# Tokens in step order, and the norm's factor multiplied at the projection's eviction

## The chip, the cores and the metric

The kernel runs on one core of one Trainium2 chip. The metric is the device time of one execution in microseconds (us). TensorE multiplies, VectorE and ScalarE work elementwise, GpSimd (POOL) and SyncE mostly move data here.

## The reference

One inference step of a two-layer hybrid decoder, for a prompt of 256 tokens and eight samples of four tokens, 288 token columns in all, model width 1024, fp32 throughout.

```python
def rmsnorm(x, g):
    y = xf * lax.rsqrt(jnp.mean(xf * xf, axis=-1, keepdims=True) + EPS)
    return (y * g).astype(x.dtype)
# layer 0: h += ab_mixer(rmsnorm(h))   latent attention + gated linear attention, w_out
# layer 1: h += s5_mixer(rmsnorm(h))   diagonal state space over positions, GELU, GLU
def channel_mixer(h, g, w_up, w_down):           # every layer
    a = jax.nn.relu(rmsnorm(h, g) @ w_up)
    return (a * a) @ w_down
def per_layer_embedding(h, p, g, w_gate, w_proj): # every layer
    gate = jax.nn.sigmoid(rmsnorm(h, g) @ w_gate)
    return gate * (p @ w_proj)
```

## The kernel before

The residual h lies in `hT` as eight tiles of 128 features by 288 tokens. A projection sums, for each block of 128 outputs, over the eight tiles in one PSUM bank. The stream of weights comes in units of 1 MB (128 x 2048) through a ring of five buffers; an up unit holds two output blocks, a down unit half a block.

Five projections (input, up 0, GLU, up 1, down 1 and the last gates) are split: each fp32 operand is written as a high part, rounded to fp32r, and a low part, the rest, and each tile takes three fast matmuls, high by high, low by high, high by low (`project_split`). ScalarE writes the high part of a weight unit (`hi_unit`), VectorE the low part (`lo_unit`), both as part of their own fixed queue, two units ahead. The high parts have three to five slots of their own.

All order is written out by hand: each engine has one program, and semaphores carry "bank full" (`result`), "bank read" (`copied`, `evacuated`) and the like. The PSUM banks are given out in a fixed order by `plan()`: the "main" groups take banks 0 to 3 in turn, so a group waits until the group four before it has been read by all of its readers.

A norm runs at a seam: ScalarE squares the eight tiles into four slots of `sq`, TensorE sums them with a matrix of 1/1024 (eight fp32 matmuls, `sumsq`, number k of the norm in `("ss", k)`), ScalarE makes the factor `rs` (logarithm, exponential), VectorE multiplies h by gain and factor, ScalarE writes the high part of the result, VectorE the low part. Norms 0, 1, 4 and 5 feed split projections; norm 1 stands before up 0, 4 before up 1, 5 before the last gates.

Up block i is read twice: ScalarE's relu writes `a2`, then VectorE multiplies `a2` by the bank. Down 0 reads `a2` as fp32; in layer 1 ScalarE and VectorE split `a2` too. While up 0 runs, VectorE also prepares the S5 coefficients (`s5_prepare`), with up blocks handled in between. After down 0 come the S5 "lag products" G, then the gated embedding (`proj`, `gate`) with the transposes `BT` and the shifted inputs `u`, then the scan of S5: VectorE scans eight groups i, TensorE makes inputs `v5` and outputs `y5`, ScalarE applies GELU (`mixed`). The GLU's input is split from `n3`. S5 works on tokens by step within a group of four (column j of step i), so before the change h is read with a stride of four there, and the GLU's result is added with a stride.

## Time and profile before

| | |
|---|---|
| median of 3 runs | 1150.16 us (1148.03 to 1151.51) |
| the profiled execution | 1150.72 us, span 1149.0 us |
| TensorE busy | 1065.5 us |
| VectorE busy | 544.2 us |
| ScalarE busy | 413.1 us |
| GpSimd busy | 140.2 us |
| mean granted TensorE clock | 0.941 |

Busy times are of the span; matmul ends are modelled, so TensorE's busy time says where it had work, not that it was at its peak. The granted clock is a share of 2.4 GHz: 1.00 is 2.4 GHz and 0.50 is 1.2 GHz.

### The profile page before, as it was taken

How to read it: one execution, taken by the hardware profiler on the slowest of the kernel's cores; microseconds unless marked ns; L12 is line 12 of the kernel's file. 1: busy time of each engine (PE TensorE's matmuls, PEld its weight loads, DVE VectorE, ACT ScalarE, POOL GpSimd, SP SyncE). 2: the span in 40 equal slices, each digit the busy share in tenths (PEclk: the TensorE clock that was granted, in tenths of full speed). 3: DMA queues.
4: the chain of work that ended last, by engine and by line, in shares of the span. 5: the costliest groups of instructions: out<-in, count | busy, mean ns of one | idle time of the engine just before them, and what ended most of it. 6: DMA issues, size and time to landing. Idle time of an engine off the chain costs nothing.

```text
span 1149.0 us, 16457 instructions
## 1 busy us (share of the span) xinstructions
PE 1065.5 (93%) x6334; PEld 882.1 (77%) x6334; DVE 544.2 (47%) x956; ACT 413.1 (36%) x714; POOL 140.2 (12%) x236
## 2 busy tenths in 40 slices
PE   6998979999999868999999998989599899999988
PEld 5996446566655546999977777758498899999978
DVE  5432665564453322986430004339564665643453
ACT  5423434431122202665140005323454545523253
POOL 3440000000034230000210007800000000000000
PEclk9997979997789979999999999989599999999999
DMA  7546001210235513344432331040044244433431
GB/s 300 169 153 233 5 1 42 69 47 19 92 119 171 151 59 134 111 163 168 147 129 103 134 147 75 1 192 1 1 156 159 89 168 161 170 147 147 157 136 42
DMA packets 33614, 134.08 MB, mean 117 GB/s; under 512 B 5241, under 2 KB 16761, under 8 KB 20994
## 3 DMA queue, kind: packets, MB, share of 16 engines
q1 hardware_dynamic: 26642, 115.53, 28.2%
q0 software_dynamic: 6896, 17.51, 4.6%
q8 instruction: 50, 0.82, 0.3%
q14 instruction: 26, 0.21, 0.1%
HBM read 128.86 MB, written 4.17 MB: 116 GB/s over the span
## 4 chain that ended last, share of the span: by engine, by line
PE 74%; DVE 13%; ACT 6%; issue 5%; POOLq 1%; DMA 1%; POOL 1%; DVEq 0%; ACTq 0%
PE ps L769 17%; PE ps L750 11%; PE ps L751 11%; PE ps L752 11%; PE ps L929 8%; PE ps L724 2%; DVE ring_split L1632 1%; DVE arena L1970 1%; PE ps L932 1%; PE ps L834 1%; DVE nT L1643 1%; PE ps L994 1%; POOLq L597 1%; ACT up_hi_split L1284 1%; PE ps L1037 1%
## 5 line engine op out<-in xcount | busy, mean ns | idle before, releaser
L929 PE MATMUL ps<-arena 128*128 128x512 f32 x256 | 150.8, 681 | 0.0
L769 PE MATMUL ps<-arena,ring 128*128 128x288 f32 x512 | 125.1, 406 | 0.0
L769 PEld LDWEIGHTS ps<-arena,ring 128*128 128x128 f32 x512 | 97.2, 190 | 26.8
L1632 DVE TENSOR_TENSOR ring_split<-ring,hi_split 128x2048 fp32r<-128x2048 f32 x37 | 84.6, 2291 | 53.0 <-ACT hi_split L1284 53.0
L932 PEld LDWEIGHTS ps<-arena 128*128 128x128 f32 x256 | 51.9, 203 | 68.2 <-issue 68.2
L750 PE MATMUL ps<-nhi_split,hi_split 128*128 128x288 f32 x320 | 96.8, 302 | 5.7 <-DVE nT_split L1636 4.6
L751 PE MATMUL ps<-nT_split,hi_split 128*128 128x288 f32 x320 | 95.0, 297 | 0.0
L752 PE MATMUL ps<-nhi_split,ring_split 128*128 128x288 f32 x320 | 94.7, 296 | 0.0
L1261 ACT ACTIVATE sq<-hT 128x288 f32<-128x288 f32 x48 | 20.6, 441 | 184.7 <-DVE hT L1919 150.9
L1919 DVE TENSOR_TENSOR hT<-hT,ps 128x288 f32<-128x288 f32 x24 | 10.9, 454 | 159.0 <-PE ps L769 129.0
L1284 ACT ACTIVATE hi_split<-ring 128x2048 fp32r<-128x2048 f32 x37 | 70.4, 1908 | 35.6 <-DMA ring<-in_stream 35.6
L1752 DVE TENSOR_REDUCE arena<-arena 128x8 f32<-128x512 f32 x64 | 43.5, 685 | 82.7 <-ACT arena L1359 82.7
L750 PE MATMUL ps<-up_nhi_split,up_hi_split 128*128 128x288 f32 x256 | 77.3, 302 | 5.4 <-DVE nT_split L1636 4.3
L751 PE MATMUL ps<-nT_split,up_hi_split 128*128 128x288 f32 x256 | 76.1, 297 | 0.0
L752 PE MATMUL ps<-up_nhi_split,ring_split 128*128 128x288 f32 x256 | 75.8, 296 | 0.0
L750 PE MATMUL ps<-a2hi_split,hi_split 128*128 128x288 f32 x256 | 75.8, 296 | 0.0
L751 PE MATMUL ps<-a2lo_split,hi_split 128*128 128x288 f32 x256 | 75.5, 295 | 0.0
L752 PE MATMUL ps<-a2hi_split,ring_split 128*128 128x288 f32 x256 | 75.3, 294 | 0.0
L1359 ACT ACTIVATE arena<-ps 128x512 f32<-128x512 f32 x64 | 38.0, 595 | 100.8 <-PE ps L929 97.2
L750 PEld LDWEIGHTS ps<-nhi_split,hi_split 128*128 128x128 f32 x320 | 60.5, 189 | 8.7 <-issue 5.2
L769 PE MATMUL ps<-nT,ring 128*128 128x288 f32 x256 | 64.2, 409 | 1.7 <-ACT arena L1507 1.3
L769 PEld LDWEIGHTS ps<-nT,ring 128*128 128x128 f32 x256 | 48.9, 192 | 15.8 <-issue 1.8
(360 smaller groups left out, 2342.2 us busy)
## 6 DMA issues: line engine op xcount, KB each, us to landing
ring<-in_stream SPq DMA_DIRECT2D x97, 1024.0 KB, 5.0
arena<-in_ckvT SPq DMA_DIRECT2D x64, 128.0 KB, 2.0
arena<-in_ckv POOLq DMA_DIRECT2D x49, 128.0 KB, 2.7
arena<-in_wu POOLq DMA_DIRECT2D x1, 2176.0 KB, 11.0
arena<-in_s POOLq DMA_DIRECT2D x4, 512.0 KB, 3.9
out_gla_s<-arena POOLq DMA_DIRECT2D x4, 512.0 KB, 2.9
arena<-in_ckv SPq DMA_DIRECT2D x15, 128.0 KB, 2.7
hT<-in_x SPq DMA_DIRECT2D x2, 576.0 KB, 4.4
```

The lines of the kernel that those rows point to most:

```text
L724: mm = pe.matmul(ps[:, 0:T], o1024, sq3[:, b % 4], start=b == 0, stop=b == DB - 1)
L750: pe.matmul(ps[:, 0:T], wh[:, k, col:col + P], xh, start=first and k == which[0], stop=False)
L751: pe.matmul(ps[:, 0:T], wh[:, k, col:col + P], xl, start=False, stop=False)
L752: mm = pe.matmul(ps[:, 0:T], wl[:, k, col:col + P], xh, start=False, stop=last and k == which[-1])
L769: mm = pe.matmul(ps[base:base + m, 0:T], wv[:, k, col:col + m], rhs(k), start=first and k == 0, stop=last and k == blocks - 1)
L929: mm = pe.matmul(ps[:, :], pages[:, p % 4, j, k], wuk[:, k], start=k == 0, stop=k == KB - 1)
L932: mm = pe.matmul(sc[:, 32 * j:32 * j + 32], pages[:, p % 4, j, k], qabs[:, k, b], start=False, stop=j == 1 and k == KB - 1, skip_group_che ...
L1261: act.activation(sq3[:, b % 4], h3[:, b], ACT.Square).then_inc(sq_ready, 1)
L1284: act.activation(hi_part(v)[:, :], ring[SPLITS[v] % RING][:, :], ACT.Copy).then_inc(hi_ready, 1)
L1359: act.activation(ksq[:, n % 2].rearrange("p h n -> p (h n)"), ps[:, :], ACT.Square).then_inc(bank_of(name), 1)
L1632: V.tensor_tensor(lo_parts[slot][:, :], ring[slot][:, :], as_whole(hi_part(v)[:, :]), ALU.subtract).then_inc(unit_split, 1)
L1752: V.tensor_reduce(ssq[:, (k + j) * NS + b], ksq[:, j], AX.X, ALU.add).then_inc(ksum_ready, 1)
```

## The change

- All tokens are in step order from the output projection on: x is loaded a second time as `x_by_step`, the mixer's outputs are written in that order, p and y are permuted on the host, and S5 reads contiguous columns. The fourth sum (k = 3) comes out as four rows of 72 columns.
- For norms 1, 4 and 5 (`LATE`) h times gain alone is split (`gained_hi`, `gained_lo`), tile by tile, as soon as a tile of h is final. The factor `rs` is multiplied where the result is read: for up in one VectorE step, maximum with 0 and then times `rs`, and ScalarE squares `a2` in place; for the last gates a VectorE step before the exponential.
- The first four output blocks take seven tiles, then the sum of squares, then the eighth tile. The squares are added on VectorE (`add_squares`), so TensorE sums two tiles, not eight.
- The GLU's first two units are split in halves after the scan; layer 1 has four slots of high parts; the lag products are in two pieces; `turns` gives the transposes out earlier; norm 2 stands on VectorE after G3.

```diff
-HI = (3, 3, 3, 5)
+HI = (3, 3, 3, 4)
+LATE = (1, 4, 5)
 def turns(i):
-    return range(3 * i, min(3 * i + 3, 16))
+    return range(3 * i + 1 if i else 0, min(3 * i + 4, 16))
...
-            main(("up", L, i), 2)
+            main(("up", L, i))
...
+        if L == 1:
+            for name in (("proj", 1, 0), ("proj", 1, 1), ("gate", 1, 0), ("gate", 1, 1)):
+                main(name)
+        for i in range(2 * L, 8):
             main(("proj", L, i))
             main(("gate", L, i), 1)
...
+            sp.wait_ge(n_ready, DB)
+            sp.dma_start(hT[:, :], ins["x_by_step"]).then_inc(x_again, 16)
...
+            def up_first_units(L, rhs, use):
+                for last in range(2):
+                    for u in range(2):
+                        w = split_unit(f"up{L}_{u}")
+                        for c in range(2):
+                            project_split(("up", L, 2 * u + c), w, P * c, 256, rhs, split_wait(use) if u == c == 0 else None,
+                                          blocks=range(7, 8) if last else range(7), first=last == 0, last=last == 1)
+                    if not last:
+                        sumsq_of_two(1 + 3 * L)
...
-            def relu(L, i):
+            def squared_up(L, i):
                 if L == 0:
                     hi_unit(min(U["up0_0"] + i // 2 + 2, U["up0_15"]))
-                ps = result(act, ("up", L, i))
-                act.activation(a2[:, i], ps[:, 0:T], ACT.Relu).then_inc(bank_of(("up", L, i)), 1)
+                copied(act, ("up", L, i))
+                act.activation(a2[:, i], a2[:, i], ACT.Square).then_inc(a_squared, 1)
...
             for b in range(DB):
+                gained_hi(1, b, prm("g_mlp0"), up_nhi)
                 square(1, b)
...
             for i in range(FB):
                 hi_unit(U["up1_0"] + i // 2 + 2)
-                relu(1, i)
+                squared_up(1, i)
                 if i:
                     a_hi_part(i - 1)
...
             def up_split(i):
                 if i < FB:
                     lo_unit(U["up1_0"] + i // 2 + 2)
                     ps = result(dve, ("up", 1, i))
-                    copied(dve, ("up", 1, i), 1)
-                    V.tensor_tensor(a2[:, i], a2[:, i], ps[:, 0:T], ALU.mult).then_inc(bank_of(("up", 1, i)), 1)
+                    V.scalar_tensor_tensor(a2[:, i], ps[:, 0:T], 0.0, rs[:, :], ALU.max, ALU.mult).then_inc(bank_of(("up", 1, i)), 1)
                 if i:
                     dve.wait_ge(a_hi, i)
                     V.tensor_tensor(a2lo[:, i - 1], a2[:, i - 1], as_whole(a2hi[:, i - 1]), ALU.subtract).then_inc(a_split, 1)
...
+                    if normed:
+                        ps = result(dve, gates[i])
+                        V.tensor_tensor(e, ps[:, 0:T], rs[:, :], ALU.mult).then_inc(bank_of(gates[i]), 1)
...
-                if i == 6:
-                    for b in range(4):
-                        n_lo(2, b, glu_nhi)
-                    lo_unit(U["glu0"])
-                if i == 7:
-                    lo_unit(U["glu1"])
+            lo_half(0, 0)
+            for b in range(4):
+                n_lo(2, b, glu_nhi)
+            lo_half(1, 0)
+            lo_half(0, 1)
             for b in range(4, DB):
                 n_lo(2, b, glu_nhi)
+            lo_half(1, 1)
```

The first place is up 1 on ScalarE. In the rows of the kernel before L1284 is the high part of a weight unit, L1434 the relu, L1582 the high part of `a2`; in the changed kernel they are L1347, the square L1497 and L1654. Before:

```order
L1284 ACTIVATE hi_split<-ring 128x2048 [waits unit_in3]
L1434 ACTIVATE arena<-ps 128x288 [waits main_ready]
L1582 ACTIVATE a2hi_split<-arena 128x288 [waits evacuated2]
L1434 ACTIVATE arena<-ps 128x288 [waits main_ready]
L1582 ACTIVATE a2hi_split<-arena 128x288 [waits evacuated3]
L1284 ACTIVATE hi_split<-ring 128x2048 [waits unit_in4]
```

and now:

```order
L1347 ACTIVATE hi_split<-ring 128x2048 [waits unit_in3]
L1497 ACTIVATE arena<-arena 128x288 [waits evacuated3]
L1654 ACTIVATE a2hi_split<-arena 128x288 [waits a_squared]
L1497 ACTIVATE arena<-arena 128x288 [waits evacuated0]
L1654 ACTIVATE a2hi_split<-arena 128x288 [waits a_squared]
L1347 ACTIVATE hi_split<-ring 128x2048 [waits main_ready,unit_in4]
```

The first step of a block waited for TensorE (`main_ready`) and now waits for VectorE's read of the bank (`evacuated`).

The second place is the same stage on VectorE: L1632 and L1702 the low part of a unit, L1935 the multiply by the bank and L2018 the step with the factor, L1938 and L2021 the low part of `a2`. Before:

```order
L1632 TENSOR_TENSOR ring_split<-ring,hi_split 128x2048 [waits hi_ready]
L1935 TENSOR_TENSOR arena<-arena,ps 128x288 [waits evacuated3,main_ready]
L1938 TENSOR_TENSOR a2lo_split<-arena,a2hi_split 128x288 [waits a_hi]
L1935 TENSOR_TENSOR arena<-arena,ps 128x288 [waits evacuated0,main_ready]
L1938 TENSOR_TENSOR a2lo_split<-arena,a2hi_split 128x288 [waits a_hi]
```

and now:

```order
L1702 TENSOR_TENSOR ring_split<-ring,hi_split 128x2048 [waits hi_ready]
L2018 SCALAR_TENSOR_TENSOR arena<-ps,rs 128x288 [waits main_ready]
L2021 TENSOR_TENSOR a2lo_split<-arena,a2hi_split 128x288 [waits a_hi]
L2018 SCALAR_TENSOR_TENSOR arena<-ps,rs 128x288 [waits main_ready]
L2021 TENSOR_TENSOR a2lo_split<-arena,a2hi_split 128x288 [waits a_hi]
```

The order is the same; the eviction no longer waits for ScalarE.

The third place is VectorE at the end of the scan: L2101 and L2197 are the scans, L2107 and L2203 the turning back, L1636 and L1706 the low parts of the GLU's input. Before:

```order
L2101 SCALAR_TENSOR_TENSOR const<-arena,const 128x256 [waits x_start,wfin_ready]
L2101 SCALAR_TENSOR_TENSOR const<-arena,const 128x256
L1632 TENSOR_TENSOR ring_split<-ring,glu_hi_split 128x2048 [waits hi_ready]
L2107 TENSOR_TENSOR sq<-const,arena 128x512 [waits scan_ready]
L2107 TENSOR_TENSOR sq<-const,arena 128x512
L2113 TENSOR_TENSOR arena<-sq 128x4x63 [waits pow_done]
L2114 TENSOR_TENSOR arena<-sq 128x4x63
L1636 TENSOR_TENSOR nT_split<-nT,glu_nhi_split 128x288 [waits n_hi] x4
```

and now:

```order
L2197 SCALAR_TENSOR_TENSOR const<-arena,const 128x256 [waits x_start,wfin_ready]
L2197 SCALAR_TENSOR_TENSOR const<-arena,const 128x256
L2203 TENSOR_TENSOR sq<-const,arena 128x512 [waits scan_ready]
L2203 TENSOR_TENSOR sq<-const,arena 128x512
L2209 TENSOR_TENSOR arena<-sq 128x4x63 [waits pow_done]
L2210 TENSOR_TENSOR arena<-sq 128x4x63
L2234 TENSOR_TENSOR ring_split<-ring,glu_hi_split 128x1024 [waits hi_ready]
L1706 TENSOR_TENSOR nT_split<-nT,glu_nhi_split 128x288 [waits n_hi] x4
L2234 TENSOR_TENSOR ring_split<-ring,glu_hi_split 128x1024 [waits hi_ready] x2
L1706 TENSOR_TENSOR nT_split<-nT,glu_nhi_split 128x288 [waits n_hi] x4
L2234 TENSOR_TENSOR ring_split<-ring,glu_hi_split 128x1024 [waits hi_ready]
```

The splits of the GLU's units stand behind the last states, in halves.

## Rows read from the trace of the kernel before

**Rows 1.** The page: the span, and busy us (share) xinstructions of each engine.

```profile
span 1149.0 us, 16457 instructions
...
PE 1065.5 (93%) x6334; PEld 882.1 (77%) x6334; DVE 544.2 (47%) x956; ACT 413.1 (36%) x714; POOL 140.2 (12%) x236
```

**Rows 2.** Waits: engine, line, whom for; us in total, times, longest.

```profile
PE ps L750 <- DVE nT_split L1636: 13.2, 4, 4.4
```

**Rows 3.** Timeline at norm 1: start us, us, engine, line, operation, count, [idle before].

```profile
451.57 4.04 PE L724 MATMUL ps<-sq,ones 128*128 128x288 f32 x16
...
463.64 0.51 DVE L1643 SCALAR_TENSOR_TENSOR nT<-hT,par,rs 128x288 f32<-128x288 f32 x1
...
465.67 0.29 PE L750 MATMUL ps<-up_nhi_split,up_hi_split 128*128 128x288 f32 x1
```

**Rows 4.** Windows: length, busy PE, PEld, DVE, ACT, POOL, PEclk, DMA share, GB/s.

```profile
745.00:750.00 5.00, 4.32 (x15) 2.54 (x16) 0.62 (x2) 0.44 (x1) 0.00 (x0) 0.66 0.01 3
...
835.00:883.90 48.90, 48.90 (x367) 48.69 (x365) 30.43 (x33) 23.73 (x30) 1.62 (x3) 1.00 0.47 164
...
900.30:997.00 96.70, 96.70 (x728) 96.70 (x727) 58.50 (x75) 49.96 (x77) 0.00 (x0) 1.00 0.47 162
```

**Rows 5.** The page's groups: count | busy us, mean ns | idle before, releaser.

```profile
L1632 DVE TENSOR_TENSOR ring_split<-ring,hi_split 128x2048 fp32r<-128x2048 f32 x37 | 84.6, 2291 | 53.0 <-ACT hi_split L1284 53.0
...
L1284 ACT ACTIVATE hi_split<-ring 128x2048 fp32r<-128x2048 f32 x37 | 70.4, 1908 | 35.6 <-DMA ring<-in_stream 35.6
```

**Rows 6.** Timeline in up 0, ScalarE, VectorE, and TensorE's end of it.

```profile
501.66 1.28 ACT L1487 ACTIVATE arena<-arena 64x512 f32<-64x512 f32 x2 [4.26 <-DVE arena L2023]
...
504.92 2.29 DVE L1632 TENSOR_TENSOR ring_split<-ring,up_hi_split 128x2048 fp32r<-128x2048 f32 x1 [2.93 <-ACT up_hi_split L1284]
...
507.49 2.14 DVE L1970 TENSOR_TENSOR arena<-arena 128x512 f32<-128x512 f32 x3
...
566.56 0.65 PE L769 MATMUL ps<-arena,ring 128*128 128x288 f32 x2
```

**Rows 7.** Timeline in up 1, one unit, ScalarE and then VectorE.

```profile
936.33 1.91 ACT L1284 ACTIVATE hi_split<-ring 128x2048 fp32r<-128x2048 f32 x1
...
942.39 0.44 ACT L1582 ACTIVATE a2hi_split<-arena 128x288 fp32r<-128x288 f32 x1
...
938.27 2.29 DVE L1632 TENSOR_TENSOR ring_split<-ring,hi_split 128x2048 fp32r<-128x2048 f32 x1 [1.24 <-ACT hi_split L1284]
...
942.60 0.46 DVE L1935 TENSOR_TENSOR arena<-arena,ps 128x288 f32<-128x288 f32 x1 [1.31 <-ACT arena L1434]
```

**Rows 8.** Timeline of TensorE at gate 0, the shifted inputs and S5's first inputs.

```profile
705.65 4.12 PE L769 MATMUL ps<-nT,ring 128*128 128x288 f32 x16 [1.33 <-ACT arena L1507]
...
745.68 1.20 PE L1146 MATMUL ps<-hT,const 128*32 128x288 f32 x8 [2.23 <-DVE arena L2063]
...
766.49 3.38 PE L1192 MATMUL ps<-arena 128*128 128x72 f32 x16 [2.74 <-DVE arena L2073]
```

**Rows 9.** Timeline at the scan's end: gelu, scan, TensorE's waits for the last states.

```profile
801.44 1.67 ACT L1550 ACTIVATE nT<-ps 32x288 f32<-32x288 f32 x4
...
805.07 1.27 DVE L2101 TENSOR_TENSOR_SCAN const<-arena,const 128x256 f32<-128x256 f32 x2
...
817.62 0.67 PE L1206 MATMUL ps<-arena 128*128 128x71 f32 x2 [9.19 <-DVE arena L2114]
...
827.01 0.67 PE L1206 MATMUL ps<-arena 128*128 128x71 f32 x2 [4.03 <-DVE arena L2114]
```

**Rows 10.** Timeline: the strided add of the GLU's last block.

```profile
885.91 0.70 DVE L1953 TENSOR_TENSOR hT<-hT,tmp 128x288 f32<-128x288 f32 x1
```

**Rows 11.** Timeline of TensorE from norm 5 to the end.

```profile
1101.89 4.04 PE L724 MATMUL ps<-sq,ones 128*128 128x288 f32 x16
...
1120.11 0.40 PE L750 MATMUL ps<-phi_split,hi_split 128*128 128x288 f32 x1 [1.56 <-DVE tmp L1948]
...
1144.08 0.29 PE L752 MATMUL ps<-nhi_split,ring_split 128*128 128x288 f32 x1
```

316 lines of the change are left out of this document (201 added, 115 removed).

## Prediction

> **What bounds the kernel now.** I read the page first, then who TensorE waits for. TensorE is busy 1065.5 of 1149.0 us, VectorE 544.2 and ScalarE 413.1 [rows 1]: TensorE is the bound, and what the change can win is the idle time between its stages. Its waits sit at the seams: the split norms alone hold 13.2 us in four waits [rows 2], and the rest is at the scan, the gates and the last layer. So I read each seam by timeline, and the long stages by windows. Inside up projection 1 TensorE has no gap: 728 matmuls in 96.7 us at granted clock 1.00 [rows 4], 0.133 us each, so one F block (24 matmuls) takes 3.2 us and one weight unit (two blocks) 6.4 us. The unit prices on the other engines are 2.29 us for a low part of a unit on VectorE and 1.91 for a high part on ScalarE [rows 5].
>
> **What the steady state hides.** In up 1 VectorE starts its split at 938.27 and ScalarE at 936.33 [rows 7], and both repeat every 6.4 us. VectorE waits twice in each unit, 1.24 for the high part and 1.31 for ScalarE's relu. ScalarE's relu needs only TensorE, so the queues keep TensorE's time; that slack is what the change spends.
>
> **The change part by part.** Times below are on the clock of the profiled execution, whose own time is 1150.72 us (1.7 around its span), 0.56 above the median 1150.16.
>
> *Layout by steps.* The four contexts copies for one, and the strided writes of eight tiles before the output projection, cost something between 0 and 3 us; the strided add of the gated unit, which the change straightens, took 0.70 us [rows 10] against 0.46 for a straight step of the same size [rows 7], so a strided write costs some 0.25 more. Most of it lies under the page work. I take +0.7. The reload of x lands long before the first add and is taken at nothing; its cover is the whole attention; without it, it would cost about what one unit of weights takes to land, 5 us by my estimate.
>
> *Norm 1.* From the end of the output projection to the second block of up 0 TensorE now needs 451.57 to 465.67, 14.1 us for 3.2 us of matmuls [rows 3]; 4.04 of it are eight sums of squares. After: seven of eight tiles of four blocks (84 matmuls, 11.2 us) run at once, then two sums (0.97), while VectorE and ScalarE finish tile 7 by 454.3. Off TensorE's path: 9.9 us.
>
> *Up 0.* Here the gain is given back. Before, ScalarE's relu read PSUM as soon as TensorE was done and went on to the next high part, while VectorE multiplied. Now VectorE goes first and ScalarE squares what VectorE wrote, so the high part of unit n+2 waits for VectorE's eviction of unit n-1's second block. The loop is: high part 1.95, low part 2.2, eviction 0.42 and 0.51, square 0.45, then the next high part: 5.6 us without the S5 preparation, which adds two steps of 2.1 us on VectorE per three blocks and two pairs of copies, 1.28 each, on ScalarE [rows 6]. I walked the three queues row by row (a step starts when its engine is free and its signal is 0.05 us old, the lengths as above). For the kernel before this walk gives VectorE's low part of unit 7 at 504.9 with its wait of 2.9, as the trace has it, and TensorE's end at 566.3 against 566.6 [rows 6]. For the changed queues it gives that low part at 506.4, though the stage began 10 us ahead; TensorE, never more than four banks ahead, waits 1.2 to 2.4 us before about every second block, 17.4 us in all, and ends up 0 at 572.8. Norm and up 0 together: +6.2 us instead of -9.9.
>
> *Between down 0 and the scan.* The sums of tiles 6 and 7 go between the two halves of the lag products, into a wait; but the norm (eight steps of at most 0.51 [rows 3]) now stands on VectorE before its copy for G4, and gate 0 needs G4's bank, which freed it at 705.6 [rows 8] and now at 705.9: +0.3. In the gates, turn 5 no longer holds a transposed block, so the shifted inputs do not wait for VectorE's copy: 2.23 us, and 1.6 for the clock, granted 0.66 in the five us around it [rows 4]: -3.8. The third sum of squares comes out already in rows of 72 columns, so one short logarithm and one exponential stand for a logarithm of 288 columns and four exponentials: about half of the wait of 2.74 goes [rows 8], 1.3, and as I take it most of the slow stretch behind it: -2.3, bounds 0 and -4.
>
> *Scan to GLU.* VectorE now waits in its scan loop for ScalarE's high parts twice, and TensorE waits 9.19 and 4.03 us for the last two groups of states [rows 9]. Of the GLU's 384 matmuls 367 lie in 835.0 to 883.9 [rows 4], so its 96th ends at 845.4. After, the loop runs on: last scan 812.4 (scan 6 ends at 806.3 [rows 9]; to it one loop of 5.2, as the sum of its steps, and 0.8 for ScalarE's reader), then on ScalarE two groups of gelu (1.67 each [rows 9]) and two high parts alternate; half a low part (1.15) opens the GLU at 817.8. 96 matmuls take 12.8, and I add 1.6 for a stretch at half clock: 832.3. -13.0.
>
> *Norm 4 and up 1.* Before: from 883.9 the 24 first matmuls last to 900.3, where the even stretch begins [rows 4], 13.2 us lost. After, the last unit of the GLU hangs: ScalarE does hi of tile 6, waits for the second adding of squares, squares, then makes the high part of up 1's second unit; VectorE its low part; only then the multiply of gate 7. Tile 6 is there 3.6 us after TensorE wants it. Then 1.0 for the sums, and when the four blocks are full the factor is there but the low part of the third unit stands before the first eviction on VectorE: 1.95 + 2.2 + 0.5, 4.3 us of wait. With 1.6 for the clock after the first wait: 10.4 lost, -2.8. In steady state the loop is now closed end to end: high 1.95, low 2.20, eviction 0.55, square 0.48, high part of the block before 0.50, its low part 0.36, eviction 0.55, square 0.48, high part 0.37: 7.4 us per unit where TensorE wants 6.4 [rows 5, 7]. TensorE then waits 0.9 to 1.0 once per unit, released by the eviction four blocks back; over the units that four banks don't cover: +10.7. The same queue is late for the first units of down 1 (0.5 and 2.1, and part of a clock dip): +3.4.
>
> *Norm 5.* Before, 240 matmuls (32.0 us) take 42.3. After, the four banks are held by two values and two gates whose last tile comes late; the third value waits for the first chain (multiply, three ScalarE steps, multiply: 2.3), the third gate for the second (2.1), one more 0.8; with 1.0 for sums and 0.8 for the clock 7.0 are lost, and the last chain is 0.6 longer [rows 11]: -2.7.
>
> Sum: +0.7 +6.2 +0.3 -3.8 -2.3 -13.0 -2.8 +10.7 +3.4 -2.7 = -3.3. From the median: 1150.2 - 3.3 = 1147 us.
>
> **Bounds.** The factor at the eviction (maximum, then multiply, out of PSUM) is in no row; it lies between 0.46 (the multiply [rows 7]) and 0.70 (the strided add); nearest is the norm's own three-operand step, 0.51 [rows 3], which I take. At 0.70 both loops grow by 0.4 per unit: +9. A square is no dearer than a copy of the same size, 0.44 [rows 7]. If the loop of up 1 were 0.3 shorter per unit, -4. The half clock at GLU's entry: none (-1.6) to all 96 matmuls (+11).
>
> **Rivals.** (1) *The loops do not bind*: TensorE stays four banks ahead in both up stages. For it speaks that VectorE is busy only 58.5 and ScalarE 50.0 of 96.7 us there [rows 4]; against it that every step of the loop waits for the one before. It would take away 17.4 + 10.7 + 4.3 + 3.4: 1111 us. (2) *Slower, by the clock*: place, up 1; TensorE now pauses once in a unit. If each pause draws a slow stretch like the one of 745 to 750 [rows 4], 1.7 us a unit against a pause of 1.0, the surplus 0.7 is paid by the fourteen units, and as much at the entries of up 1 and down 1: +10, 1157 us. It decides as soon as the stretch costs more than the pause. For it: that stretch followed a wait of 2.23 [rows 8]; against it: after 1.56 us in the last gates the matmul took 0.40 as others do at full clock [rows 11]. The Trainium skill, page "TensorE: Matmul & The Clock Gate", section "A second HAM failure mode: psum-queue depth-cycling", has a kernel whose pauses between groups of matmuls, while it cycled through banks, made the clock oscillate. By that rule this rival would come true; the trace shows falls after longer pauses only. (3) *Scan to GLU gives little*: ScalarE's order there is as long as before, the clock stays at 0.50 through the first two units: -2 instead of -13, 1158 us. (4) *Partly bound*: the walk overstates the loops by a third: -10 more, 1137 us.
>
> **How the numbers follow.** The forecast has 0.57, with its own range 1141 to 1153; (1) 0.08, (2) 0.10, (3) 0.08, (4) 0.17. A difference under 0.3% (3.5 us) can't be told from none. Of the forecast's 0.57, 0.24 lie below 1146.7, 0.30 between, 0.03 above 1153.6. Of (4) 0.02 lie within 0.3%. Faster 0.24 + 0.08 + 0.15 = 0.47; same 0.30 + 0.02 = 0.32; slower 0.03 + 0.10 + 0.08 = 0.21. Leaving (1) and the far ends out gives 1134 to 1158.
>
> **What would show it.** Right: TensorE idle near 1 us once per unit in up 1, released by VectorE's eviction, units 7.3 to 7.5 us apart; idle 1 to 2.5 us in up 0, which ends later against the end of the output projection by 6; no 9 us wait before the GLU; waits of about 2 us for banks at the third value and gate. Wrong: up units 6.4 us apart (then 1111), a granted clock under 0.9 in up 1 (then 1157), or GLU's first matmul later than 10 us after the last scan.

## The result, and the profile after

The changed kernel takes 1159.12 us (median of 5 executions, 1158.72 to 1163.06); the kernel before, run beside it, 1150.41 (1148.03 to 1151.86). The ratio is 1.0102, with a 95% interval of 1.0078 to 1.0126: slower by about 1%, where 0.3% faster was forecast. The profiled execution took 1163.06 us, with a span of 1161.4, 12.4 more than the span in [rows 1]. It is the slowest of the five, so the differences read from it below add up to 12.4 us, where the medians differ by 8.7.

The page after, with the span, the busy times, and the granted clock in 40 slices (tenths):

```profile
span 1161.4 us, 16430 instructions
...
PE 1078.4 (93%) x6346; PEld 899.5 (77%) x6346; DVE 545.8 (47%) x954; ACT 414.8 (36%) x711; POOL 138.8 (12%) x236
...
PEclk9997979897799989999999999965599899999999
```

TensorE is busy 13 us longer with about the same work. The clock row says where: the slices with a 6 and two 5s are 755 to 842 us, the scan.

I set the times of TensorE's stages in the two traces side by side. The output projection starts at 420.43 us before and 420.42 after and is as long, so whatever differs behind it comes from the stages behind it. What the changed kernel's trace has for each term of the prediction:

| stretch | forecast | measured |
|---|---|---|
| layout ahead of the output projection | +0.7 | 0.0 |
| norm 1 and up 0 | +6.2 | +6.3 |
| lag products, gate 0, gates, shifted inputs | +0.3 - 3.8 = -3.5 | -3.8 |
| last sum of the third norm to the scan's first inputs | -1.3 of the -2.3 | -1.7 |
| scan and GLU | -13.0 and the other -1.0 | +10.0 |
| norm 4, up 1, down 1 | -2.8 + 10.7 + 3.4 = +11.3 | +2.7 |
| norm 5 to the end | -2.7 | -1.1 |
| sum | -3.3 | +12.4 |

Two stretches are off: the scan by 24 us to the bad, up 1 by 9 to the good. TensorE at the scan's entry, after:

```profile
765.53 0.33 PE L740 MATMUL ps<-sq,ones 128*32 128x72 f32 x8 [2.22 <-ACT sq L1318]
767.35 3.66 PE L1237 MATMUL ps<-arena 128*128 128x72 f32 x16 [1.49 <-DVE arena L2169]
770.94 1.19 PE L1184 MATMUL ps<-hT,const 128*32 128x288 f32 x8
```

The two waits (2.22 and 1.49) are together no longer than those of the kernel before (1.36 and, in [rows 8], 2.74). Both kernels lose the clock at about 767 us. In the kernel before it is back at 773.6; in the changed one it stays at 0.50 for 78 us, until GLU. Windows of the kernel before and then of the changed one, columns as in [rows 4]:

```profile
766.80:773.60 6.80, 6.80 (x36) 5.72 (x35) 4.19 (x11) 0.87 (x4) 0.00 (x0) 0.50 0.60 251
775.00:780.00 5.00, 5.00 (x43) 3.68 (x39) 5.00 (x14) 0.72 (x4) 0.00 (x0) 1.00 0.02 5
```

```profile
770.00:775.00 5.00, 5.00 (x27) 3.95 (x26) 3.62 (x10) 0.76 (x4) 0.00 (x0) 0.50 0.70 292
835.00:840.00 5.00, 5.00 (x26) 5.00 (x25) 3.03 (x6) 4.57 (x7) 0.00 (x0) 0.50 0.00 0
845.00:897.00 52.00, 52.00 (x391) 52.00 (x391) 33.29 (x43) 32.55 (x50) 1.62 (x3) 1.00 0.45 157
```

In the changed kernel TensorE has work without a gap in the first two windows (5.00 of 5.00) and still runs at 1.2 GHz; with GLU the clock returns.

The scan goes in groups, and three engines take part in each. Two groups of TensorE in the kernel before (from inputs to inputs), and then in the changed one (from outputs to outputs):

```profile
794.36 1.95 PE L1192 MATMUL ps<-arena 128*128 128x72 f32 x16
...
798.83 1.95 PE L1192 MATMUL ps<-arena 128*128 128x72 f32 x16
```

```profile
804.75 1.91 PE L1245 MATMUL ps<-arena 128*128 128x72 f32 x8
...
813.28 1.91 PE L1245 MATMUL ps<-arena 128*128 128x72 f32 x8
```

TensorE's own work for such a group takes 4.47 us before (798.83 - 794.36) and 8.53 after (813.28 - 804.75). But the pace of the scan is not TensorE's in both. VectorE's scans of the same groups, before:

```profile
794.51 1.27 DVE L2101 TENSOR_TENSOR_SCAN const<-arena,const 128x256 f32<-128x256 f32 x2
...
799.90 1.26 DVE L2101 TENSOR_TENSOR_SCAN const<-arena,const 128x256 f32<-128x256 f32 x2
```

and after, with VectorE's wait for TensorE (through ScalarE's copy):

```profile
805.01 1.27 DVE L2197 TENSOR_TENSOR_SCAN const<-arena,const 128x256 f32<-128x256 f32 x2
...
812.20 0.43 DVE L2188 TENSOR_TENSOR const<-const,tmp 128x256 f32<-128x256 f32 x1 [3.05 <-ACT arena L1599]
...
813.53 1.27 DVE L2197 TENSOR_TENSOR_SCAN const<-arena,const 128x256 f32<-128x256 f32 x2
```

Before, VectorE scans a group every 5.39 us (799.90 - 794.51) and is busy 12.97 of the 13 us from 790 to 803: it sets the pace, and TensorE has slack. At half clock TensorE's group is the longer one, VectorE waits for it, and the groups come 8.52 us apart (813.53 - 805.01). From the scan's first inputs to GLU's first matmul the kernel before takes 63.9 us (830.42 - 766.49), with the waits of 9.19 and 4.03 of [rows 9] in it; the changed one, without these waits, takes 74.9 (842.25 - 767.35).

TensorE's waits after, in up 0 (L2011) and up 1 (L2018: total us, times, longest), and then those of up 1 by timeline: for tile 6, at the third unit, and once per unit later:

```profile
PE ps L776 <- DVE arena L2011: 14.1, 10, 2.1
...
PE ps L776 <- DVE arena L2018: 6.5, 8, 4.2
```

```profile
899.02 0.40 PE L776 MATMUL ps<-nhi_split,hi_split 128*128 128x288 f32 x1 [1.72 <-DVE up_lo_split L1711]
...
914.76 0.58 PE L776 MATMUL ps<-nhi_split,hi_split 128*128 128x288 f32 x1 [4.16 <-DVE arena L2018]
...
962.35 0.37 PE L776 MATMUL ps<-nhi_split,hi_split 128*128 128x288 f32 x1 [0.18 <-DVE arena L2018]
969.34 0.37 PE L776 MATMUL ps<-nhi_split,hi_split 128*128 128x288 f32 x1 [0.37 <-DVE arena L2018]
976.34 0.37 PE L776 MATMUL ps<-nhi_split,hi_split 128*128 128x288 f32 x1 [0.37 <-DVE arena L2018]
```

In up 0 the waits are near the forecast: ten of at most 2.1 us, 14.1 in all, where 17.4 was forecast. In up 1 there is one wait per unit, released by VectorE's eviction, as forecast, but it is 0.37 us and not near 1, and the units are 7.00 us apart (976.34 - 969.34), not 7.4.

### The profile page after: what moved, and what is told of

Read it like the earlier page. It is cut to its first block, busy times and chain, and to the rows that moved or that the text cites. A ratio compares the mean times of both kernels' runs of the same rounds, so it can differ in the third digit from the quotient of the medians.

```text
span 1161.4 us, 16430 instructions
## 1 busy us (share of the span) xinstructions
PE 1078.4 (93%) x6346; PEld 899.5 (77%) x6346; DVE 545.8 (47%) x954; ACT 414.8 (36%) x711; POOL 138.8 (12%) x236
## 4 chain that ended last, share of the span: by engine, by line
PE 68%; DVE 15%; ACT 10%; issue 5%; POOLq 1%; DMA 1%; POOL 1%; DVEq 0%; ACTq 0%
PE ps L807 17%; PE ps L776 8%; PE ps L967 7%; PE ps L778 7%; PE ps L777 7%; DVE ring_split L1702 5%; ACT hi_split L1347 3%; PE ps L1237 2%; PE ps L1245 1%; PE ps L1252 1%; PE ps L1251 1%; ACT up_hi_split L1347 1%; ACT a2hi_split L1654 1%; PE ps L970 1%; DVE arena L2018 1%
## 5 line engine op out<-in xcount | busy, mean ns | idle before, releaser
L1702 DVE TENSOR_TENSOR ring_split<-ring,hi_split 128x2048 fp32r<-128x2048 f32 x36 | 82.3, 2292 | 56.6 <-ACT hi_split L1347 56.6
L776 PE MATMUL ps<-up_nhi_split,up_hi_split 128*128 128x288 f32 x256 | 77.5, 303 | 14.1 <-DVE arena L2011 14.1
L777 PE MATMUL ps<-up_lo_split,hi_split 128*128 128x288 f32 x256 | 76.6, 299 | 0.0
L777 PE MATMUL ps<-up_lo_split,up_hi_split 128*128 128x288 f32 x256 | 76.2, 298 | 0.0
L1347 ACT ACTIVATE hi_split<-ring 128x2048 fp32r<-128x2048 f32 x36 | 68.4, 1906 | 8.1 <-DMA ring<-in_stream 8.0
L1497 ACT ACTIVATE arena<-arena 128x288 f32<-128x288 f32 x64 | 28.0, 446 | 114.2 <-DVE arena L2018 57.1
```

The lines of the kernel that those rows point to most:

```text
L776: pe.matmul(ps[:, 0:T], wh[:, k, col:col + P], xh, start=first and k == which[0], stop=False)
L777: pe.matmul(ps[:, 0:T], wh[:, k, col:col + P], xl, start=False, stop=False)
L1347: act.activation(hi_part(v)[:, :], ring[SPLITS[v] % RING][:, :], ACT.Copy).then_inc(hi_ready, 1)
L1497: act.activation(a2[:, i], a2[:, i], ACT.Square).then_inc(a_squared, 1)
L1702: V.tensor_tensor(lo_parts[slot][:, :], ring[slot][:, :], as_whole(hi_part(v)[:, :]), ALU.subtract).then_inc(unit_split, 1)
```

## The experiments

Theory A: the scan is slow because TensorE's granted clock falls ahead of it and its own, now lighter, work does not bring it back. A second form of it, A' in the expectations: the scan's own matmuls don't even hold the clock where it is at 1.00 when the scan begins. Theory B: the new order of ScalarE's and VectorE's work slows the scan, and the clock only follows. Theory C: in the up projections the loop of eviction, square and next high part holds TensorE back, as predicted.

The table has every run. The fourth column is the profiled execution from the start of the output projection to the end of the span. That start lies between 415.2 and 425.9 us in these traces, in kernels that do the same ahead of it, so single times and spans differ by some us for a reason that is none of the experiments'; where one profile is set against another I use this column. It is 728.6 us for the kernel before and 741.0 for the changed one. Kernels between two lines ran on one chip and share the runs of the kernel before (its medians there: 1147.75, 1149.78, 1149.39 and 1150.02). The changed kernel itself (ratio 1.0102) was not run again with them, so the others are compared with it by ratio or by the fourth column.

| run | median us (lowest to highest) | ratio to before, 95% interval | from the output projection on |
|---|---|---|---|
| `warm_short` | 1154.04 (1150.74 to 1156.20) | 1.0045, 1.0021 to 1.0070 | 733.8 |
| `warm_long` | 1173.16 (1168.65 to 1173.44) | 1.0199, 1.0162 to 1.0235 | 751.0 |
| `squares_late` | 1148.89 (1143.15 to 1154.94) | 0.9995, 0.9971 to 1.0018 | 727.4 |
| `shifted_twice` | 1141.80 (1140.54 to 1143.19) | 0.9949, 0.9926 to 0.9973 | 718.6 |
| --- | | | |
| `after_strided` | 1142.64 (1139.69 to 1147.69) | 0.9948, 0.9929 to 0.9966 | 718.5 |
| `before_straight` | 1164.79 (1162.22 to 1166.94) | 1.0131, 1.0101 to 1.0162 | 745.3 |
| `late_twice` | 1126.66 (1123.94 to 1130.17) | 0.9798, 0.9769 to 0.9827 | 706.7 |
| `late_twice_third` | 1117.55 (1115.82 to 1122.68) | 0.9721, 0.9697 to 0.9745 | 700.2 |
| --- | | | |
| `strided_in_scan` | 1141.94 (1139.67 to 1144.76) | 0.9941, 0.9921 to 0.9961 | 720.1 |
| `strided_in_gates` | 1163.78 (1162.13 to 1164.44) | 1.0127, 1.0097 to 1.0157 | 740.8 |
| `kept_twice` | 1128.74 (1124.55 to 1130.39) | 0.9820, 0.9783 to 0.9857 | 707.7 |
| `kept_once` | 1139.56 (1137.93 to 1140.29) | 0.9913, 0.9884 to 0.9941 | 717.0 |
| --- | | | |
| `wide_once` | 1141.65 (1139.18 to 1147.58) | 0.9913, 0.9892 to 0.9934 | 720.0 |
| `kept_fit` | 1115.98 (1111.35 to 1117.90) | 0.9713, 0.9693 to 0.9732 | 694.5 |
| `kept_wide` | 1116.62 (1116.40 to 1116.76) | 0.9708, 0.9691 to 0.9726 | 694.5 |

### Keeping TensorE at work ahead of the scan

```diff
+            def keep_busy(ps, n):
+                for _ in range(n):
+                    pe.matmul(ps[:, 0:T], ident, h3[:, 0], start=True, stop=True, skip_group_check=True)
+            keep_busy(bank(("v5", 0)), 10)
             sumsq_part(3, 7)
...
+            keep_busy(bank(("v5", 0)), 12)     # warm_long: 48
```

Expected of `warm_short`:

> The changed kernel, with TensorE kept at work in the two idle stretches ahead of the scan: 10 matmuls of 288 columns ahead of the last sum of squares of the third norm (it waited 2.22 us there) and 12 ahead of the scan's first matmul (1.49 us), into a bank that the scan's first group overwrites. They leave nothing out. Theory A (the scan is slow because TensorE's granted clock falls to 0.50 after these two waits and its own work does not bring it back): the clock stays above 0.9 from 766 to 840 us, a group of the scan takes about 5.35 us as before instead of 8.53, GLU opens some 25 us sooner, and the time is 1159 - 22 = 1137 us, at most 1145. Theory B (the scan loop is slower by the new order of the work on ScalarE and VectorE): groups stay over 7 us apart whatever the clock, and the time is 1158 to 1160. Theory A' (the scan's own matmuls are too thin to hold the clock): the clock falls all the same, some us into the scan, and the time is 1150 to 1160.

Expected of `warm_long`:

> As the short one, but with 48 matmuls of 288 columns ahead of the scan's first matmul instead of 12 (6.4 us at full clock, 4 to 5 of them beyond the wait). Theory A: the clock is at 1.00 when the scan begins and stays there; GLU opens 25 - 5 = 20 us sooner than in the changed kernel, time 1139 to 1143. If the short filling was too short, this one alone shows the gain. Theory B: 1159 + 4 = 1163. Theory A': the clock falls inside the scan whatever ran ahead of it, 1155 to 1164.

Neither came out as A asked. `warm_short` (1154.04) lies in the range of A', 1150 to 1160; `warm_long` (1173.16) is slower than the changed kernel and outside all three ranges. The trace of `warm_short` shows two reasons. The filling, and later TensorE's waits inside the scan:

```profile
760.57 5.12 PE L1227 MATMUL ps<-hT,const 128*128 128x288 f32 x20
...
765.88 6.09 PE L1227 MATMUL ps<-hT,const 128*128 128x288 f32 x24
...
788.15 1.11 PE L1251 MATMUL ps<-arena 128*128 128x72 f32 x8 [0.89 <-DVE arena L2175]
...
794.41 1.97 PE L1251 MATMUL ps<-arena 128*128 128x72 f32 x8 [1.08 <-DVE arena L2175]
```

Each of these matmuls is two instructions and 0.51 us, four times what I had counted, so ten took 5.12 us for a wait of 2.22; the 48 of `warm_long` took 23.6, which is why it is slower. And from 766 to 794 us the clock was 1.00, with TensorE's matmuls short (1.11 for the first of two rows above, 1.97 at half clock for the other); then, after waits of 0.89, 0.31 and 1.08 us, it fell and did not return until GLU. While it was at 1.00, VectorE's scans came 5.4 us apart (775.7, 781.1, 786.5), later 8.3 and 9.9 (803.5, 811.8, 821.7). So B is out: with the same order on the other engines, the groups follow the clock. What A left out is that TensorE at full clock has so little to do in a group that it waits for VectorE, and that the clock fell after such waits.

### One part of the layout alone: how the shifted inputs read h

The change reads h straight where the kernel before reads every fourth column. `after_strided` puts the stride back into the changed kernel, `before_straight` takes it out of the kernel before; both do work of the same size, on other columns of h than the reference has.

```diff
-                                   h3[:, b:b + 4, J * t:J * t + J], start=True, stop=True, skip_group_check=True)
+                                   h3[:, b:b + 4].rearrange("p b (j i) -> p b i j", i=TS)[:, :, t], start=True, stop=True, skip_group_check=True)
```

Expected of `after_strided`:

> The changed kernel, with one thing as before: the 64 matmuls of the shifted inputs read h with a stride of four columns, not straight (h lies by steps now, so the values that they take are others; nothing is left out, the work is of the same size). They then take 1.20 us for 8 at full clock instead of 0.67. Theory of the straight reads (they made TensorE's work after the fall lighter, so its clock no longer comes back): the clock comes back to 1.00 near 773 us as in the kernel before, groups of 5.4 to 6 us, time 1140 to 1148 against 1156 to 1159 of the changed kernel. Rival (the exact idle times ahead of the scan decide, and they are as in the changed kernel: 2.22 and 1.49): the clock stays at 0.50 and the time is that of the changed kernel, 1156 to 1160.

Expected of `before_straight`:

> The kernel before, with the shifted inputs read straight (the columns 72 t to 72 t + 72 of h, which are other tokens in this layout; same size of work). Theory of the straight reads: here too the clock, which before came back at 773 us, stays at 0.50 until GLU, groups go from 5.35 to 8.5 us, and the time is 1165 to 1172. Rival (the idle times decide): TensorE's waits ahead of the scan are as before, the clock comes back, and the time is 1145 to 1150, slightly less than before.

This one access pattern turns both kernels over: the changed one goes from 1.0102 to 0.9948, the one before from 1 to 1.0131. About the same five us in the two traces, `after_strided` by timeline (the inputs x16 take 2.68 instead of 3.7, since the clock returns in them) and `before_straight` by window:

```profile
770.22 1.22 PE L1184 MATMUL ps<-hT,const 128*32 128x288 f32 x8
771.37 2.68 PE L1237 MATMUL ps<-arena 128*128 128x72 f32 x16
773.98 1.20 PE L1184 MATMUL ps<-hT,const 128*32 128x288 f32 x8
```

```profile
770.00:775.00 5.00, 5.00 (x27) 3.95 (x26) 4.45 (x11) 0.76 (x4) 0.00 (x0) 0.50 0.00 0
```

Neither run settles the rival, that the idle times decide: with shorter shifted inputs between the gates TensorE waits 1.86 us instead of 1.36 in `before_straight`, and 1.69 instead of 2.22 in `after_strided`. So the next two runs tell the place apart: the stride in the five shifted inputs inside the scan alone, and in the three between the gates alone (again other columns of h).

```diff
+                    if i >= 3:      # strided_in_gates: i < 3
+                        x = h3[:, b:b + 4].rearrange("p b (j i) -> p b i j", i=TS)[:, :, t]
```

Expected of `strided_in_scan`:

> The changed kernel, with the stride only in the five shifted inputs of the scan; the three between the gates read straight (values differ, nothing is left out). At half clock 8 such matmuls take 1.22 us strided and 1.19 straight, so what makes the clock return can't be their length there. If the work after the fall decides, the clock returns near 773 us and the time is 1140 to 1146. If the work ahead of the fall decides (the shifted inputs between the gates), it stays at 0.50: 1156 to 1160.

Expected of `strided_in_gates`:

> The counterpart: the stride only in the three shifted inputs between the gates, ahead of the fall; those of the scan read straight. The work after the fall decides: clock 0.50 until GLU, 1156 to 1160. The work ahead of it decides: 1140 to 1146. If both this and its counterpart return to full clock, or neither does, the clock hangs on the sum of both or on exact times, and that stays open.

The work after the fall decides: 0.9941 with the stride in the scan, 1.0127 with it in the gates (1163.78 us, above the 1156 to 1160 expected, but 740.8 in the fourth column, as the changed kernel's 741.0). And the idle times do not: `strided_in_scan` waits 2.23 and 1.48 us ahead of the scan, as the changed kernel does (2.22 and 1.49), and `strided_in_gates` 1.70 and 1.48, as `after_strided` does (1.69 and 1.48), each with the other outcome. Nor is it an accident of the profiled executions: all 7 of `strided_in_scan` lie between 1139.67 and 1144.76, all 4 of `strided_in_gates` and all 5 of the changed kernel between 1158.72 and 1164.44. TensorE in `strided_in_scan`, and then in `strided_in_gates`:

```profile
768.42 1.22 PE L1187 MATMUL ps<-hT,const 128*32 128x288 f32 x8
769.57 2.53 PE L1239 MATMUL ps<-arena 128*128 128x72 f32 x16
```

```profile
771.01 1.19 PE L1187 MATMUL ps<-hT,const 128*32 128x288 f32 x8
772.13 3.69 PE L1239 MATMUL ps<-arena 128*128 128x72 f32 x16
```

### More work in the same place

```diff
                 if i + 6 < 8:
+                    for t in range(TS):     # shifted_twice
+                        pe.matmul(bank(("u", i + 6))[32 * t:32 * t + 32, 0:4 * J], ident[:, 0:32], h3[:, 0:4, J * t:J * t + J], start=True, stop=True,
+                                  skip_group_check=True)
+                    pe.matmul(bank(("u", i + 6))[:, 0:T], ident, h3[:, 0], start=True, stop=True, skip_group_check=True)     # wide_once, instead
                     shifted(i + 6)
```

Expected of `shifted_twice`:

> The changed kernel, with each of the five shifted inputs inside the scan loop (8 matmuls of 288 columns with 32 rows out) issued twice; nothing is left out. In the kernel before the same 8 read h with a stride and took 1.20 us at full clock, now 0.67. Theory A with thin work (TensorE's clock did come back in the scan before, at about 773 us, because more of its time there went to wide matmuls): the clock comes back to 1.00 within the first five groups, groups 5.4 to 6 us, time 1135 to 1150. Theory A without it (once fallen, the clock is not brought back by a little more of the same): each repeat costs 1.2 us at half clock, 1159 + 6 = 1165. Theory B: VectorE's queue is not touched and TensorE has slack at full clock, no more than 1160 either way.

Expected of `wide_once`:

> The changed kernel, with one matmul of all 128 rows and 288 columns (two instructions, 0.51 us at full clock as the filling of the first run showed, so about 1 at half) ahead of each of the five shifted inputs in the scan, instead of a repeat of the whole shifted input (which took 0.51 us more at full clock). The stride brought the clock back without making the matmuls longer at half clock (1.22 against 1.19), so length alone is not the reason. If any more work of TensorE's in these groups is enough, the clock returns near 773 us and the time is 1140 to 1143. If it has to be several rows' groups side by side, or reads of h, as in the repeat and in the stride, it stays at 0.50 and the time is 1159 + 5.

Both bring the clock back, with no stride, for work that nobody needs: 22.4 and 21.0 us less than the changed kernel in the fourth column (of the 22.4, 1.3 lie in up 0 and 1.2 in the last layer, which the edit does not touch). In `wide_once`, before the return and behind it:

```profile
776.24 1.26 PE L1260 MATMUL ps<-hT,const 128*128 128x288 f32 x2
777.42 1.19 PE L1184 MATMUL ps<-hT,const 128*32 128x288 f32 x8
778.54 2.04 PE L1237 MATMUL ps<-arena 128*128 128x72 f32 x16
```

So it needs neither the stride nor matmuls side by side. A little more work per group was enough: one wide matmul, 1.2 us at half clock and 0.6 at full. In each of the runs whose clock came back in this way it fell again, for 17 us, at TensorE's waits of 0.8 to 2.2 us for the last groups.

### The closed loop of the up projections

```diff
             def squared_up(L, i):
                 if L == 0:
                     hi_unit(min(U["up0_0"] + i // 2 + 2, U["up0_15"]))
+                    i -= 1
...
             for i in range(FB):
                 hi_unit(U["up1_0"] + i // 2 + 2)
-                squared_up(1, i)
-                if i:
-                    a_hi_part(i - 1)
+                if i:
+                    squared_up(1, i - 1)
+                if i > 1:
+                    a_hi_part(i - 2)
...
-                if i:
-                    dve.wait_ge(a_hi, i)
-                    V.tensor_tensor(a2lo[:, i - 1], a2[:, i - 1], as_whole(a2hi[:, i - 1]), ALU.subtract).then_inc(a_split, 1)
+                if i > 1:
+                    dve.wait_ge(a_hi, i - 1)
+                    V.tensor_tensor(a2lo[:, i - 2], a2[:, i - 2], as_whole(a2hi[:, i - 2]), ALU.subtract).then_inc(a_split, 1)
```

In up 1 the high part of a block on ScalarE and its low part on VectorE both move one block later.

Expected of `squares_late`:

> The changed kernel, with ScalarE's order in both up projections turned back to what it was: the high part of unit n+2 ahead of the square of the block before, and in up 1 the high part of a block one block later still. Theory C (the closed loop eviction, square, next high part holds TensorE back in up 0): the 14.1 us of waits in up 0 fall to under 4, units of up 1 come 6.4 to 6.6 us apart instead of 7.0; time 1159 - 10 - 7 = 1142 us, if the scan's clock stays as it is. Rival: VectorE's longer queue alone (eviction with the preparation of the scan) holds TensorE: then up 0 gains under 3 us, up 1 nothing, and the time is 1154 to 1160. The scan's groups should still take 8.5 us at clock 0.50; if they come out at 5.35 here, the start of the stage decides the clock by its exact times, and Theory A is too simple.

In the changed kernel up 0 ends 152.3 us after the start of the output projection, here 144.1. Up 1 has no wait behind the two at its entry (1.6 and 4.2 us): TensorE works 90.00 of 90 us, where the changed kernel had 87.64 in the same window. The waits in up 0 of `squares_late`, and then its window in up 1:

```profile
PE ps L776 <- DVE arena L2017: 7.9, 8, 1.7
```

```profile
920.00:1010.00 90.00, 90.00 (x677) 90.00 (x676) 53.25 (x67) 46.00 (x69) 0.00 (x0) 1.00 0.44 154
```

It is 13.6 us less in the fourth column (741.0 to 727.4): 7.6 ahead of the scan, 4.3 in up 1 and 1.8 in down 1. In up 1 theory C holds as it was stated. In up 0 it holds for about half: the waits fell from 14.1 to 7.9 us, not to under 4, and the time is 1148.89, not 1142. The scan stayed at half clock, as expected. The 7.9 us that remain in up 0 stand beside the preparation of the scan on VectorE, which the rival names; what they hang on was not tried.

### The parts together

`late_twice` is `squares_late` and `shifted_twice` in one. `late_twice_third` also makes the high and the low part of up 1's third unit ahead of the factor:

```diff
             h_parts(8)
+            hi_unit(U["up1_2"])
             rsqrt(rs[:, :], ("ss", 4))
...
             add_squares(4, 2)
+            lo_unit(U["up1_2"])
             copied(dve, ("ss", 4))
```

Expected of `late_twice`:

> The changed kernel with the high part of unit n+2 ahead of the square again in both up projections, and the shifted inputs in the scan issued twice. If the two effects are of different places, they add: 1141.8 less the 12.7 us of up 0 and the 6 of up 1, 1123 us; down to 1130 if up 1 gives less. If the clock's return depends on the time at which the scan begins and not on TensorE's work alone, it may stay at 0.50 here: 1146 to 1150, no better than the later squares alone.

Expected of `late_twice_third`:

> As the one before, and the high and low part of up 1's third unit made ahead of the factor of the fourth norm, while both engines wait for its sums (ScalarE is idle for 9.6 us there, VectorE for 11.6). The wait of 4.16 us for a bank at the third unit, and the half clock behind it (some 1.6 us), go: 5 to 6 us less than the one before, about 1118. Rival: the tile 6 wait just ahead or the next low part takes it over, and no more than 2 us are gained.

The first gave 706.7 us in the fourth column; 741.0 less 13.6 and less the 22.4 of `shifted_twice` would be 705.0, so the two effects add within 2 us. (The 12.7 us that I had expected of up 0 alone held 5.2 of an earlier start of the output projection; 7.6 is right.) The third unit gave another 6.5 there, and 9 in the medians: the wait of 4.16 us is gone, with the half clock behind it. Up 1 and down 1 then have no wait of TensorE over 0.6 us behind the one for tile 6.

Then the waits after which the clock fell, ahead of the scan and in its last groups, were filled. `kept_once` is `kept_twice` without the repeated shifted inputs, `kept_fit` has a third of the fillings, and `kept_wide` is `kept_fit` with one wide matmul per group in place of the repeat:

```diff
+            def keep_busy(ps, n):
+                for _ in range(n):
+                    pe.matmul(ps[0:32, 0:4 * J], ident[:, 0:32], h3[:, 0:4, 0:J], start=True, stop=True, skip_group_check=True)
+            keep_busy(bank(("v5", 0)), 12)                     # kept_fit: 4
             sumsq_part(3, 7)
+            keep_busy(bank(("v5", 0)), 8)                      # kept_fit: 3
...
                 ps = bank(("y5", i))
+                keep_busy(ps, {5: 6, 6: 18}.get(i, 0))         # kept_fit: 2 and 6
...
                     sample_states(i + 2)
+                    if i == 5:
+                        hi_unit(U["glu0"])
                     last_states(i + 2)
```

Expected of `kept_twice`:

> Later squares, shifted inputs of the scan twice, up 1's third unit ahead of the factor (1117.6 us), and now TensorE kept at work in four waits: 24 matmuls of 288 columns and 32 rows out, 2.0 us, in the wait of 2.22 ahead of the third norm's last sum, 16 (1.3) in the wait of 1.48 ahead of the scan, 12 (1.0) and 36 (3.0) in the waits of 1.03 and 2.22 us of its last groups; and ScalarE makes the high part of GLU's first unit ahead of the last states of group 7 (it is idle for 2.6 us there). If the falls of the clock follow from these waits, it stays at 1.00 from 750 to 825: 3.4 us less at the entry of the scan, 3 to 5 less at GLU's, time 1109 to 1112. If the entry gains nothing because VectorE bounds the scan at full clock, 1112 to 1114. If the fillings are too thin to hold the clock, 1117 or more.

Expected of `kept_once`:

> As the one before, with the shifted inputs of the scan issued once. In the run with short filling the clock held until TensorE waited 0.89, 0.31 and 1.08 us inside the scan, then stayed at 0.50. If it needs the repeated matmuls not only to return but to be held, the clock falls near 785 us and the time is 10 to 16 us longer than with them, 1121 to 1128. If keeping TensorE at work ahead of the scan is enough, the time is that of the one before, less up to 1 us.

Expected of `kept_fit`:

> The version with TensorE kept at work, with the fillings a third as long: the last run showed that one matmul of 288 columns with 32 rows out takes 0.25 us when it stands alone (5.74 for 23), where I had counted 0.084 from the shifted inputs (8 in 0.67, side by side). Now 8 instructions (2.0 us) in the wait of 2.22, 6 (1.5) in that of 1.48, 4 (1.0) and 12 (3.0) in the scan's last groups. If the 11 us that the last run lost were the surplus length of the fillings, the clock stays at 1.00 from 750 to 825 us and the time is 1108 to 1112. If a full clock at the entry and the end of the scan is worth nothing since VectorE bounds it there, 1115 to 1118, as without fillings. If the shorter fillings don't hold the clock, 1117 to 1122.

Expected of `kept_wide`:

> As the one before, with the one wide matmul per group instead of the repeated shifted input. If the wide one is as good for the clock, the same time within 2 us. If not, the clock falls near 785 us, as with the shifted inputs once, and the time is 10 to 14 us longer.

In `kept_twice` the clock was 1.00 from 750 to 830 us and the kernel still took 11 us more in the medians than `late_twice_third`, 7.5 in the fourth column. The filling ahead of the third norm's last sum shows why:

```profile
753.06 5.74 PE L1227 MATMUL ps<-hT,const 128*32 128x288 f32 x23
```

0.25 us for an instruction, where the same shape in the shifted inputs takes 0.084 (8 in 0.67). The shifted inputs write four different groups of 32 rows and run side by side; mine all wrote one group. The Trainium skill, page "TensorE: Matmul & The Clock Gate", section "Part 3: Packing small matmuls — row/col tiling", says that small matmuls overlap when they stand in different tiles of the array; 0.25 us in one group of rows against 0.084 over four agrees with it. With a third of the filling (`kept_fit`) the stretch from the output projection on is 694.5 us, 5.7 less than without fillings (the earlier high part of GLU's first unit is in this too). The clock is 1.00 in the whole scan; three of its windows:

```profile
750.00:755.00 5.00, 4.62 (x39) 2.00 (x28) 2.03 (x5) 2.16 (x6) 0.00 (x0) 1.00 1.02 426
770.00:775.00 5.00, 5.00 (x52) 4.23 (x51) 4.22 (x12) 3.54 (x9) 0.00 (x0) 1.00 0.00 0
800.00:805.00 5.00, 4.57 (x38) 4.46 (x38) 4.05 (x9) 4.81 (x9) 0.00 (x0) 1.00 0.01 3
```

The medians do not tell it from `late_twice_third` (0.9713 and 0.9721, intervals that overlap), and 1115.98 lies in the range recorded for fillings that are worth nothing, 1115 to 1118. By the profiles the scan itself, from its first inputs to GLU, is 5.4 us shorter (48.4 for 53.9, and 48.4 in `kept_wide` too), but the profiled execution of `late_twice_third` is the slowest of its six, so a gain from the fillings is not shown. `kept_wide` is as good as `kept_fit`. `kept_once` took 1139.56 us, 10.8 more than `kept_twice` (10 to 16 were expected): the clock fell near 790 us, after waits of 0.90 and 1.08 inside the scan, so with the fillings ahead of it alone it did not hold. All six versions beat both kernels; the best take 2.9% less time than the one before.

## Why the prediction was wrong

**The step that failed is "Scan to GLU", -13.0 with the "layout by steps" at +0.7.** The layout term priced only writes. It never asked what the straight read does to the shifted inputs, though their strided rows lay in [rows 8] (1.20 us for eight), and it took TensorE's clock in the scan to be that of the kernel before, which fell and came back within 7 us. The straight read made TensorE's work there lighter (1.20 to 0.67 us for eight at full clock, 1.22 to 1.19 at half), and the clock did not come back: scan and GLU came out 24 us above their forecast, more than the whole miss of 15.7 in this profile. Norm 4, up 1 and down 1, which came out 8.6 below theirs, hid part of it by luck. With the stride put back (`after_strided`), from the third norm's last sum to the end of GLU takes 107.0 us, where the kernel before takes 120.9: 13.9 less, against 15.3 forecast. So the terms "scan to GLU" and "sums k = 3" were sound under the clock that they assumed, and GLU opens 9.7 us sooner than in the kernel before (counted from the output projection), without the wait of 9 us. None of the signs of being wrong that the prediction named came: the units of up 1 were 7.0 us apart, the clock in up 1 was 1.00, and GLU's first matmul came 9.0 us after the last scan. None of them looked at the groups of the scan.

**Norm 1 and up 0: right.** The queue walk gave +6.2, the trace +6.3. With the closed loop opened (`squares_late`) up 0 ends 8.2 us sooner, about half of what the prediction says that up 0 gives back; the cause of the other half was argued by the walk and not tested.

**Up 1: right in mechanism, too large in size.** From the end of GLU to down 1 the kernel before takes 115.6 us, the changed one 116.5 and `squares_late`, without the loop, 112.2. So the loop costs 4.3, not the 10.7 of the sum: it is 7.0 us per unit, not 7.4. One unit of it in the changed kernel, ScalarE's high part, VectorE's low part and eviction, ScalarE's square and the next high part of a block:

```profile
964.60 1.91 ACT L1347 ACTIVATE hi_split<-ring 128x2048 fp32r<-128x2048 f32 x1
...
969.23 0.44 ACT L1497 ACTIVATE arena<-arena 128x288 f32<-128x288 f32 x1 [2.73 <-DVE arena L2018]
969.58 0.43 ACT L1654 ACTIVATE a2hi_split<-arena 128x288 fp32r<-128x288 f32 x1
...
966.54 2.29 DVE L1702 TENSOR_TENSOR ring_split<-ring,hi_split 128x2048 fp32r<-128x2048 f32 x1 [1.35 <-ACT hi_split L1347]
968.74 0.45 DVE L2018 SCALAR_TENSOR_TENSOR arena<-ps,rs 128x288 f32<-128x288 f32 x1
```

The eviction with the factor costs 0.45, just under the low end of its bounds (0.46), and the next step of the same engine starts some 0.1 before the row of the one ahead ends (969.58 against 969.23 + 0.44). I had summed whole rows. The surplus over TensorE's 6.4 is then 0.6 a unit instead of 1.0, and TensorE's first wait for it comes at 962, when half of the stage is over. **Down 1** has the late first units at +1.8 instead of +3.4, from the same queue.

**Norm 4: right**, -3.4 (112.2 less 115.6) against -2.8: though of its two waits the one for tile 6 is 1.72 (3.6 forecast) and only the one for the bank, 4.16, is as forecast (4.3). **Gates and shifted inputs: right**, -3.8 against -3.5, though a new slow stretch stands at gate 0 (clock 0.69 from 710 to 715). **Norm 5: half**, -1.1 against -2.7; the two waits are there, 2.20 and 1.87 (2.3 and 2.1 forecast). Most of the miss is the clock, for which the prediction has 0.8: from the end of down 1 on the kernel before takes 47.3 us and the changed one 46.1, with the clock at half for 6.8 us there; `after_strided` and `shifted_twice`, with the same code but half clock for only 3.4 us, take 45.0 and 44.9.

**The rivals.** (1), loops that do not bind, did not come. (2), the clock in up 1, did not either: TensorE pauses 0.37 us in each unit and the clock is 1.00 from 920 to 1010. The Trainium skill, page "TensorE: Matmul & The Clock Gate", section "A second HAM failure mode: psum-queue depth-cycling", by which this rival would have come true, is not borne out here by pauses of that size. The prediction's own reading against this rival, that the trace shows falls after longer pauses only, was wrong, though. In the kernel before the clock fell at 807.8, behind a wait of 0.95 us and ahead of the one of 9.19; the outputs in which it fell took 1.32 us instead of 1.06:

```profile
805.30 0.41 PE L1206 MATMUL ps<-arena 128*128 128x71 f32 x2 [0.95 <-DVE arena L2114]
...
807.11 1.32 PE L1200 MATMUL ps<-arena 128*128 128x72 f32 x8
```

So waits near 1 us were followed by a fall in the scan, and waits of 0.37 in up 1 were not. (3) had the nearest number, 1158, for a stretch at half clock in GLU's first units; the half clock covered the scan instead, which no rival had. (4), loops overstated by a third, was right in direction: up 1 and down 1 were overstated by more (10.7 and 3.4 for 4.3 and 1.8), up 0 was not.

## What to carry to other kernels

Ask of every edit that makes TensorE's work lighter in a stretch of small matmuls whether the clock comes back there afterwards: busy time of 100% in the window does not say so, only the granted clock does. Where it does not, a few unneeded matmuls in the loop can be worth far more than they cost (here five of 0.6 us against 21), if their length is first read from a row of the same placement. Ask also which engine sets the pace of the loop at either clock: here VectorE at full clock (5.39 us a group) and TensorE at half (8.53). And when a read of PSUM passes from one engine to another, write down the loop that the engines now close together and put the step that nothing waits for, here the square, behind the one that TensorE waits for.

## What the runs showed of the hardware

- In the changed kernel TensorE stayed at 1.2 GHz for 78 us, with no idle time in its row from the scan's first inputs (767.35) to GLU (842.25), and the clock was back 2.8 us after GLU's first matmul.
- At half clock eight shifted inputs take 1.22 us strided and 1.19 straight, and the inputs between them are the same; yet in the three kernels with the stride in the scan (the one before, `after_strided`, `strided_in_scan`) the clock returned within 7 us, and in the four without it and without added matmuls (the changed one, `before_straight`, `strided_in_gates`, `squares_late`) it did not until GLU. Why is open: TensorE's row is without a gap in both, and its rows differ by 0.03 us.
- The strided read of eight shifted inputs cost time only at full clock: 1.20 against 0.67 us there, 1.22 against 1.19 at half.
- An fp32 instruction of 288 columns with 32 rows out took 0.25 us where all wrote one group of rows (`kept_twice`, 5.74 for 23) and 0.084 in a set of eight over four groups (0.67 for 8).
